# A conditioned encoder layer on one core: the ends of three projections and the start of the second FFN in two token halves

## What is computed

```
x += 0.5*g1 * swiglu(mod(rms_norm(x)))        # FFN 1, 1024 -> 2816 -> 1024
z  = mod(rms_norm(x)) @ W_in ; mixer(z)       # HGRN2 and RG-LRU heads
x += g2 * concat(heads) @ W_out               # output projection
x += 0.5*g3 * swiglu(mod(rms_norm(x)))        # FFN 2
out = rms_norm(x)
# rms_norm(x) = x / sqrt(mean over channels of x*x + eps) * gain ; mod(h) = h*(1+scale) + shift
```

## Time and profile before

| | |
|---|---|
| Median of 3 runs | 1069.49 us (1069.32 to 1071.6) |
| The profiled execution's own time | 1068.98 us |
| Its span | 1067.3 us, 13762 instructions |
| PE busy | 1045.8 us (98%) |
| Weight loads on PE | 857.5 us (80%) |
| DVE busy | 563.4 us (53%) |
| ACT busy | 416.9 us (39%) |
| POOL busy | 62.1 us (6%) |
| Chain that ended last | PE 88%, issue 6%, DVE 4%, ACT 1% |
| Granted clock of TensorE | at full speed in all 40 slices |

### The profile page before, as it was taken

The page is one execution under the profiler, slowest core; times in us unless marked ns, Lnnn a source line. Parts: engine busy times, 40 slices in busy tenths (PEclk is TensorE's granted clock), DMA queues, the critical chain, the costliest instruction groups (busy, mean ns, idle before and its releaser), DMA issues.

```text
span 1067.3 us, 13762 instructions
## 1 busy us (share of the span) xinstructions
PE 1045.8 (98%) x4920; PEld 857.5 (80%) x4920; DVE 563.4 (53%) x780; ACT 416.9 (39%) x566; POOL 62.1 (6%) x84
## 2 busy tenths in 40 slices
PE   8999999999999999999999989999999999999996
PEld 6778888888888888787788868878888888888885
DVE  4467777733423237568999995553333333322323
ACT  5242222222312124586878962442222222221211
POOL 0111112100000110000100000200000000000100
PEclk9999999999999999999999999999999999999999
DMA  9658888823332323222121202212233333322222
GB/s 358 258 180 292 284 291 288 259 97 98 99 98 99 98 81 144 79 80 80 40 80 40 78 26 76 80 64 95 97 98 98 98 98 98 98 94 90 94 97 79
DMA packets 37570, 132.95 MB, mean 125 GB/s; under 512 B 4128, under 2 KB 4384, under 8 KB 37408
## 3 DMA queue, kind: packets, MB, share of 16 engines
q1 hardware_dynamic: 29024, 100.83, 28.3%
q0 software_dynamic: 8512, 31.66, 8.7%
HBM read 130.37 MB, written 2.10 MB: 124 GB/s over the span
## 4 chain that ended last, share of the span: by engine, by line
PE 88%; issue 6%; DVE 4%; ACT 1%; POOL 0%; DMA 0%; DVEq 0%; SPq 0%; ACTq 0%; POOLq 0%
PE psum L1303 26%; PE psum L1305 26%; PE psum L1304 26%; PE psum L1593 2%; PE psum L1406 2%; PE psum L1441 1%; PE psum L1399 1%; PE psum L1532 1%; PE psum L1534 1%; PE psum L1533 1%; PE psum L1607 1%; PE psum L1561 1%; ACT whi L362 0%; PE psum L1421 0%; DVE outt L1294 0%
## 5 line engine op out<-in xcount | busy, mean ns | idle before, releaser
L362 ACT ACTIVATE whi<-raw 128x1024 fp32r<-128x1024 f32 x164 | 174.0, 1061 | 535.2 <-PE psum L1305 527.2
L757 DVE TENSOR_TENSOR wlo<-raw,whi 128x1024 fp32r<-128x1024 f32 x166 | 205.9, 1241 | 324.6 <-ACT whi L362 323.4
L1303 PE MATMUL psum<-hhi,whi 128*128 128x512 f32 x896 | 354.7, 396 | 2.7 <-DVE wlo L757 1.5
L1305 PE MATMUL psum<-hhi,wlo 128*128 128x512 f32 x896 | 349.0, 389 | 0.0
L1304 PE MATMUL psum<-hlo,whi 128*128 128x512 f32 x896 | 348.8, 389 | 0.0
L1303 PEld LDWEIGHTS psum<-hhi,whi 128*128 128x128 f32 x896 | 168.3, 188 | 43.3 <-issue 3.9
L1305 PEld LDWEIGHTS psum<-hhi,wlo 128*128 128x128 f32 x896 | 168.2, 188 | 35.3
L1304 PEld LDWEIGHTS psum<-hlo,whi 128*128 128x128 f32 x896 | 168.4, 188 | 34.7 <-issue 1.2
L1303 PE MATMUL psum<-ghi,whi 128*128 (+1 forms) x352 | 137.2, 390 | 0.0
L1305 PE MATMUL psum<-ghi,wlo 128*128 (+1 forms) x352 | 137.0, 389 | 0.0
L1304 PE MATMUL psum<-glo,whi 128*128 (+1 forms) x352 | 136.9, 389 | 0.0
(11 more groups left out here) (194 smaller groups left out, 880.4 us busy)
## 6 DMA issues: line engine op xcount, KB each, us to landing
raw<-wu SPq DMA_DIRECT2D x168, 512.0 KB, 3.4
ada<-wada POOLq DMA_DIRECT2D x56, 512.0 KB, 4.9
early<-wada SPq DMA_DIRECT2D x16, 512.0 KB, 15.2
x<-xt SPq DMA_DIRECT2D x4, 512.0 KB, 5.3
out<-outt SPq DMA_DIRECT2D x8, 256.0 KB, 2.1
bd<-bd POOLq DMA_DIRECT2D x1, 1024.0 KB, 5.0
csr<-c_rows POOLq DMA_DIRECT2D x1, 512.0 KB, 5.4
dif<-consts POOLq DMA_DIRECT2D x1, 448.0 KB, 6.2
```

Of the source, the lines that this page charges most:

```text
L362: nc.scalar.activation(whi[:, slot, :], raw[:, slot, :], ACT.Copy).then_inc(hi_done, 1)
L757: nc.vector.tensor_tensor(wlo[:, slot, :], raw[:, slot, :], whi[:, slot, :], ALU.subtract).then_inc(lo_done, 1)
L1303: nc.tensor.matmul(dst, a, rhi, start=start, stop=False)
L1305: return nc.tensor.matmul(dst, b, rhi, start=False, stop=stop)
```

## The change

The columns of x, h and the output are cut into halves of 256 tokens (`HT`, `cols(hf)`) at the three turns.

In the last two output tiles (6 and 7) of the down projections and of the output projection each half is multiplied into a bank of its own: half 0 of both tiles, then half 1 of both. In the down projections the first 14 blocks of tiles 6 and 7 stay whole; their sum is added to x by DVE (`update_part`) ahead of the last units. `update_half` adds each half, `square_half` squares it, and the column sums, the root, the reciprocal and the spread are made for each half (`half_sums_of`, `root_half`, `inverse_half`, `half_rb_of`). On PE the sums and the spread of half 0 stand between the blocks of half 1 of tiles 6 and 7. The sums and the spread of half 1 stand among the first matmuls of the next stage (turns 1 and 2) or behind four dummies each (turn 3). `norm_turn` with its dummies is gone.

Turn 1: tiles 0 to 3 of h are made in halves, tiles 4 to 7 whole; the two v units are multiplied for half 0, then for half 1. Turn 2: all eight tiles of h are made in halves, and the first two units of FFN 2 run over half 0 and then half 1, the second unit four tiles behind the first. The squares of tiles 4 and 5 are no longer added by POOL there. Turn 3: sixteen products and sixteen stores of 256 columns instead of eight of 512. Banks of v, sums and spread are other ones.

```diff
@@ up_step on PE, f == 0
-                    for t in range(KD + 2):
-                        for s, k in ((0, t), (1, t - 2)):
...
-                            ins = three(bank[2 * s], s, k * P, hhi[:, k, :], hlo[:, k, :], k == 0, k == KD - 1)
+                    for hf in range(2):
+                        for t in range(KD + 4):
+                            for s, k in ((0, t), (1, t - 4)):
...
+                                ins = three(bank[2 * s][:, cols(hf)], s, k * P, hhi[:, k, cols(hf)], hlo[:, k, cols(hf)],
+                                            k == 0, k == KD - 1)
...
+                            if hf == 0 and t == 2:
+                                half_sums_of(2, 1)
+                            if hf == 0 and t == 5:
+                                half_rb_of(2, 1)
@@ end of ffn_down on PE
+                for d in (6, 7):
+                    pe.wait_ge(lo_done, unit_of(d) + 1)
+                    last_blocks(d, 0, range(8)).then_inc(half_done, 1)
+                    if d == 7:
+                        norm_sums(norm, 1)
+                last_blocks(6, 1, range(4))
+                half_sums_of(norm, 0)
+                last_blocks(6, 1, range(4, 8)).then_inc(unit_used, 1)
+                last_blocks(7, 1, range(2))
+                half_rb_of(norm, 0)
+                last_blocks(7, 1, range(2, 8)).then_inc(unit_used, 1)
@@ PE, first units after turn 1
-            for m in range(13):
+            z_half(0, 0)
+            half_sums_of(1, 1)
+            z_half(0, 1)
+            half_rb_of(1, 1)
+            for m, hf in ((1, 0), (0, 1), (1, 1)):
+                for part in range(2):
+                    z_half(m, part, hf)
+            for m in range(2, 13):
@@ PE, end of the output projection
-            out_blocks(28, 58)
-            norm_sums(2, 0)
-            out_blocks(58, 64)
-            norm_turn(2, 2)
+            out_blocks(28, 48)
...
+            for o in (6, 7):
+                pe.wait_ge(lo_done, U_OUT + o + 1)
+                last_blocks(o, 0, range(KD)).then_inc(half_done, 1)
+            norm_sums(2, 0)
+            last_blocks(6, 1, range(4))
+            norm_sums(2, 1)
+            half_sums_of(2, 0)
...
@@ DVE, after turn 3
+            update_half(2, 6, 0)
+            update_half(2, 7, 0)
+            inverse_half(3, 0)
+            update_half(2, 6, 1)
+            for d in range(6):
+                final(d, 0)
+            update_half(2, 7, 1)
+            final(6, 0)
+            final(7, 0)
+            inverse_half(3, 1)
             for d in range(KD):
+                final(d, 1)
@@ SP
-            for d in range(KD):
...
+            for hf in range(2):
+                for d in range(KD):
+                    sp_.wait_ge(out_ready, KD * hf + d + 1)
+                    sp_.dma_start(out[d * P:(d + 1) * P, cols(hf)], outt[:, d, cols(hf)]).then_inc(stored, 16)
```

More of the change, by code:

```diff
@@ L462, in ffn_down @@
                             hi(i + v // 2, v % 2)
-                for d in range(4, KD):
-                    if d < 7:
-                        hi_u(u + PAIR_UNITS + d - 2)
+                for d in (4, 5):
+                    hi_u(u + PAIR_UNITS + d - 2)
                     square(norm, d)
-                root(norm)
-                hi_u(u + HALF_UNITS + 1)
+                turn(norm, u + HALF_UNITS)
             act.wait_ge(vecs_loaded, 32)
@@ L479, in _ @@
             rows_copy(0)
-            root(0)
+            first_root()
             hi(0, 0)
@@ L740, in _ @@
             y_upper(7)
-            for d in range(KD):
-                if d in (0, 2, 4):
+            for d in range(6):
+                if d in (0, 2):
                     hi_u(U_OUT + 6 + d // 2)
                 square(2, d)
-            root(2)
-            hi_u(U_OUT + 9)
-            h_upper(2)
+            turn(2, U_OUT + 8)
             ffn_up(1)
@@ L1340, in down_unit @@
                         ins = three(bank[(4, 0)[half] + d], slot, (4 * t + d) * P, rhi, rlo, first and t == 0,
-                                    last and t == 1)
+                                    last and t == 1 and (half == 0 or d >= 2))
                 ins.then_inc(unit_used, 1)
@@ L1384, in ffn_down @@
+                for d in (4, 5):
+                    pe.wait_ge(lo_done, unit_of(d) + 1)
                     for k in range(8):
                         rhi, rlo = rhs_of(KF - 8 + k)(0)
[L1386 removed]
+                        ins = three(bank[d - 4], unit_of(d) % 2, k * P, rhi, rlo, False, k == 7)
                     ins.then_inc(unit_used, 1)
[L1389 to L1401 removed]
+                    if d == 4:
+                        norm_sums(norm, 0)
@@ new lines, in norm_sums @@
+            def norm_sums(n, part):
+                if part == 0:
+                    pe.wait_ge(x_ready, x_at(n, 3))
+                    if n != 2:
+                        pe.wait_ge(x_part, n + 1)
+                both = n == 2 and part
+                if both:
+                    pe.wait_ge(sq_done, squares_at(n) + 6)
+                else:
+                    pe.wait_ge(sq_added, added_at(n) + 2 + part)
+                for slot in range(2 if both else 1):
+                    for c in range(TC):
+                        ins = nc.tensor.matmul(half_sums(n, c // 2)[:, c % 2:c % 2 + 1], sq[:, slot, c * P:(c + 1) * P],
+                                               ones[:, 0:1], start=(part == 0 and c % 2 == 0), stop=False,
+                                               skip_group_check=True)
+                ins.then_inc(sq_used, 1)
```

299 lines of the change are left out of this document (201 added, 98 removed).

## The result

| | Before | Changed |
|---|---|---|
| Median | 1069.51 us (1069.06 to 1071.6, 10 runs) | 1073.42 us (1072.14 to 1075.32, 10 runs) |
| Ratio, 95% interval | | 1.0035 (1.0026 to 1.0044) |
| The profiled execution, its span | 1068.98, 1067.3 us | 1072.25, 1070.5 us |
| Mean granted clock | 0.998 | 0.995 |

What follows compares the result with a forecast made beforehand. PE, busy 98% of the span, was taken as the bound, so only its streaming and three turns without real work count. The turns sum to -2.8 + 3.0 - 0.8 = -0.6 us, 1069.49 to 1068.9 us; range 1066.5 to 1072.0.

Steps and rivals of the forecast that it cites:

- Turn 1: Down projection to input projection, across the norm: the unit after the two v units starts 2.8 us earlier.
- Turn 2: Output projection to FFN 2: half 1's late chain leaves PE idle 3.0 us; 3.0 us lost in all.
- Turn 3: End of the kernel after the last down matmul: products shrink, the late chain takes part back, -0.8 us.
- What bounds the kernel: Whole kernel: PE busy 98% of the span, so only what it streams and three places without real work matter.
- Half matmuls: 192 wide matmuls become 384 of 256 columns at 0.116 us each (0.111 to 0.120), adding 1.0 us.
- Rival C: All 384 half matmuls cost well over half; at 0.15 the sum is +7.4, 1076.9 us; chance 0.12.
- Rival D: Turn 1's gain is lost in the mixer, where DVE holds PE up: +2.2, 1071.7 us; chance 0.08.
- The sum: All three turns: -2.8 + 3.0 - 0.8 = -0.6 us, so 1068.9 us.
- Rival B: Without dummies the clock falls to half in turn 2: +0.9 to +1.9, 1069.8 to 1070.8 us; chance 0.17.
- third sign of being wrong: The prediction is wrong if the granted clock drops in turn 2.

Runs made afterwards that it cites:

- filled_all: filled_both with every idle piece of PE in turn 2 covered by dummies, also ahead of tiles 0, 1 and 2 of h: 1071.85 us, ratio 1.0025.
- filled: The change with nine dummy matmuls of 128 columns between blocks 3 and 4 of the first FFN 2 unit: 1072.18 us, ratio 1.0029.
- filled_both: filled plus three dummies ahead of the first sums, and the 24 one-column passes in the output projection parted by blocks: 1074.13 us, ratio 1.0045.
- spread_early: The change with the spread of half 1 moved on PE from behind tile 5 to ahead of tile 4 of the first FFN 2 unit: 1072.57 us, ratio 1.0033.
- turn2_whole: The change with turn 2 taken back (whole tiles, dummies in), turns 1 and 3 still halved: 1066.82 us, ratio 0.998 to the kernel before.
- whole_no_dummies: turn2_whole without the 19 dummy calls between the sums, the spread and the first tile of h in turn 2: 1067.65 us, ratio 0.9985.

## Why the prediction was wrong, point by point

- **What bounds the kernel**: right. PE's real work, and three places where it has none.
- **Half matmuls**: 0.116 taken, 0.120 measured (384.70 to 384.82), my upper end. Over 384 of them that is up to 1.5 us, part of it hidden. Rival C (0.15) is out. By the formula of the Trainium skill ("TensorE: Matmul & The Clock Gate", Back-to-back issue gap) it would be 0.109, an estimate; the measured row decides.
- **Turn 1**: -2.8 predicted, -2.3 measured, sizes only: waits of 0.43 and 0.22 stand where I had 0.57 and 0.22, and 96 half matmuls at 0.120 make 0.38 of the rest. The first matmul behind small passes took 0.20 instead of 0.12 (391.27 to 391.47), which I had nowhere in the terms. Rival D is out: from turn 1 to turn 2 only 0.1 was lost (2.17 us ahead at 411.88, 2.07 at 670.31).
- **Turn 2**: +3.0 predicted, +5.4 measured. This is the step that failed: the size of turn 2's term, in which the clock stood at nothing and a half round of DVE at 0.85. The order of events was right to the row (first sums late, then waits for tiles 0 to 2, then 2.7 us of idle where I had 3.0). Two terms were off. The clock: 1.45 us in the profiled execution. I had put it at nothing because the idle piece was shorter than the one at the end of the span. The sizes: without a fall it would be +3.9. Tile 0 started at 16.96 where I had 16.5, 0.38 of it from 96 half matmuls at 0.120, and from there it is 19.8 where I had 19.3, since DVE and ACT need 0.91 us per half tile where I took 0.85 (702.34 to 703.25), eight times in a row. The error is thus 1.45 for the clock and 0.94 for sizes.
- **Turn 3**: -0.8 predicted, -0.1 measured. Products started 17.65 us after output tile 6 (I had 17.0) and took 3.2 (3.1); from there to the end of the span it is 2.8 (2.8). So the miss lies ahead of the products: 96 x 0.004 = 0.38, and a wait of 0.33 for the last square.
- **The sum**: the three turns came to 0.5 + 2.4 + 0.7 = 3.6 us more than forecast, 1.45 of it the clock; the span to 3.8 more, and the median to 4.5, for the reasons given with the result. The terms written out add up to less than my totals in places (26.4 for the 26.6 of turn 1; 15.7 for the 15.9 and 34.6 for the 34.9 of turn 2), so as written they were further off still.
- **Rival B** had 0.17, and its mechanism came, which was my third sign of being wrong. I named the place and the trigger, and its price of 0.9 to 1.9 holds the 1.45 of the profile. Its time (1069.8 to 1070.8) did not come, for it stood over a forecast that was itself 2.2 too low, and the clock alone does not make the loss: filled_all keeps it and is 2.7 above the kernel before. I did not see that the clock could come down behind the one-column sums or the waits for tiles 0 to 2 too. The argument against it ("the idle piece is shorter than that one" at the span's end) was wrong: it fell behind a piece of 2.7 us here, and in filled with PE busy for all of 680 to 685.
- The range ended at 1072.0 since I gave each size its own margin. They went the same way: a half cost more than half on PE (0.120 against 0.113) and on DVE (0.91 against 0.725).

## What to carry to other kernels

The two turns suggest a rule that two places can't prove: halving a tile pays where the consumer takes longer per piece than the producer. In turn 1 a whole tile of h feeds 12 matmuls, 2.7 us, and costs DVE 1.45, and the earlier first piece was worth 2.3 us. In turn 2 it feeds 6 (1.36 us), a half tile 0.72 against 0.91 on DVE, and the later last piece cost 3.9 us with the clock kept. So compare the two paces before a stage is cut, place by place. And before you take dummy matmuls out, ask what waits for PE behind them: their loss cost nothing in the profile behind DVE's whole tiles (some 0.4 us in single executions), and 1.45 us where DVE waited for a spread at half speed.

## What the runs showed of the hardware

- The clock fell without a long stop of PE. In filled PE was busy for all of 680 to 685, with 24 one-column sums shortly ahead of the fall at 683, and the last stop ahead of them was one of 0.6 us; in filled_both the longest stop ahead of the fall at 690.3 was 1.15 us. It stood at half for 3.4 or 6.8 us each time.
- Executions of one kernel differ in how much the clock falls: the mean clocks of the change go from 0.992 to 0.996. The place differs too where the instructions are the same: up to tile 3 of h filled is the change, and only filled fell at 683. The executions of filled, spread_early and filled_both lie 2.1, 2.5 and 4.3 us apart; the eleven of turn2_whole, whose turn 2 has its dummies, within 1.2 us. But the eleven of whole_no_dummies, all with lower clocks, lie within 1.4, and 21 of the kernel before 2.8 apart, so a fall in turn 2 is not all that spreads them.
- A half matmul took 0.120 us at full clock and 0.213 at half, one of 512 columns 0.2266 at full.
- Stores of 128 KB went out at 254 to 279 GB/s from one queue and at 291 to 349 from two; those of 256 KB before at 375 to 394 from one. The last is the pace of DVE's products (eight in 5.36 us, 391 GB/s), not a limit of the queue that these runs show.

```profile
GB/s 31 0 0 0 0 0 0 0 0 0 0 0 0 0 0 0 0 0 0 0 66 382 375 386 379 386 375 382 394 378 386 105 0 0 0 0 0 0 0 0
```
